# The halves of a weight tile made in pieces of 512 columns on GpSimd

## Time and profile before

| what | value |
|---|---|
| median of 3 runs | 2966.47 us (2964.6 to 2966.97) |
| the profiled execution | 2968.2 us, span 2966.2 us |
| mean granted TensorE clock | 0.987 |
| TensorE busy (matmuls) | 2858.6 us, 96% of the span |
| GpSimd busy | 1653.8 us, 56% |
| VectorE busy | 1540.7 us, 52% |
| ScalarE busy | 685.0 us, 23% |
| DMA | 285.48 MB, mean 96 GB/s |

### The profile page before, as it was taken

One profiled execution on the slowest core, in us unless ns is written; L12 is line 12 of the kernel. 1 busy time (PEld: TensorE's weight loads), 2 busy tenths in 40 slices (PEclk: granted clock), 3 DMA queues, 4 the chain that ended last, 5 costly groups with the idle time before them and its releaser, 6 DMA issues.

```text
span 2966.2 us, 44556 instructions
## 1 busy us (share of the span) xinstructions
PE 2858.6 (96%) x18104; PEld 2236.8 (75%) x18104; DVE 1540.7 (52%) x2279; ACT 685.0 (23%) x1169; POOL 1653.8 (56%) x1340
## 2 busy tenths in 40 slices
PE   4999998999999999999999999999999999899998
PEld 3666777888877767778888777777777777688786
DVE  5778776555224674444333375565465446462342
ACT  2444212000013442111000133233323333210001
POOL 3534567777765234576767744344435434566663
PEclk8999999999999999999999999999999999999999
DMA  7523543344323111232222221121111111222221
GB/s 242 162 101 120 181 166 136 128 153 145 131 96 92 34 59 65 70 115 81 96 99 99 101 67 54 53 69 66 48 59 69 67 53 67 78 85 92 92 100 57
DMA packets 102371, 285.48 MB, mean 96 GB/s; under 512 B 26030, under 2 KB 37038, under 8 KB 101934
## 3 DMA queue, kind: packets, MB, share of 16 engines
q1 hardware_dynamic: 85568, 274.75, 26.5%
q10 hardware_dynamic: 16622, 8.21, 1.2%
HBM read 280.76 MB, written 6.06 MB: 97 GB/s over the span
## 4 chain that ended last, share of the span: by engine, by line
PE 90%; DVE 6%; ACT 1%; issue 1%; DMA 1%; POOL 1%; ACTq 0%; DVEq 0%; SPq 0%; POOLq 0%
PE ps L334 26%; PE ps L336 24%; PE ps L335 24%; PE ps L1266 3%; PE ps L1088 3%; PE ps L1098 2%; PE ps L1108 2%; DMA raw<-in_weights_dram 1%; PE ps L1311 1%; DVE raw L1510 1%; PE ps L1408 1%; PE ps L1230 0%; PE ps L1388 0%; DVE mg L1657 0%; PE ps L1244 0%
## 5 line engine op out<-in xcount | busy, mean ns | idle before, releaser
L548 POOL TENSOR_TENSOR wR<-raw,wR 128x512 fp32r<-128x512 f32 (+1 forms) x866 | 1184.5, 1386 | 37.6
L544 POOL CAST wR<-raw 128x1024 fp32r<-128x1024 f32 (+4 forms) x470 | 475.1, 1011 | 1241.7 <-PE ps L336 1162.9
L334 PE MATMUL ps<-hR,wR 128*128 128x512 f32 x2320 | 946.2, 408 | 56.1 <-DVE hR L1552 26.7
L335 PE MATMUL ps<-hR,wR 128*128 128x512 f32 x2320 | 911.5, 393 | 0.0
L336 PE MATMUL ps<-hR,wR 128*128 128x512 f32 x2320 | 911.4, 393 | 0.0
L334 PEld LDWEIGHTS ps<-hR,wR 128*128 128x128 f32 x2320 | 440.0, 190 | 175.3 <-issue 59.0
L336 PEld LDWEIGHTS ps<-hR,wR 128*128 128x128 f32 x2320 | 439.5, 189 | 95.1
L335 PEld LDWEIGHTS ps<-hR,wR 128*128 128x128 f32 x2320 | 440.7, 190 | 87.9 <-issue 4.8
L1510 DVE CUSTOM_DVE_ANT_0 raw<-raw,cs 128x1024 f32<-128x1024 f32 x96 | 147.0, 1547 | 21.5 <-DMA raw<-in_weights_dram 13.9
L334 PE MATMUL ps<-act_f,wR 128*128 128x512 f32 x352 | 137.8, 391 | 0.0
L336 PE MATMUL ps<-act_f,wR 128*128 128x512 f32 x352 | 137.0, 389 | 0.0
(11 more groups left out here) (362 smaller groups left out, 3944.2 us busy)
## 6 DMA issues: line engine op xcount, KB each, us to landing
raw<-in_weights_dram SPq DMA_DIRECT2D x484, 512.0 KB, 3.3
raw<-in_weights_dram SPq DMA_DIRECT2D x50, 128.0 KB, 2.3
raw<-in_weights_dram SPq DMA_DIRECT2D x16, 256.0 KB, 2.6
bias_copies<-bias_rows ACTq DMA_DIRECT2D x2, 1905.0 KB, 9.1
bias<-bias_copies ACTq DMA_DIRECT2D x16, 224.0 KB, 7.2
raw<-in_weights_dram SPq DMA_DIRECT2D x8, 384.0 KB, 5.0
xT<-in_x_dram SPq DMA_DIRECT2D x1, 2048.0 KB, 9.2
out_dram<-xT SPq DMA_DIRECT2D x4, 512.0 KB, 2.7
```

The source lines that it names most:

```text
L334: mm(out, w_hi, r_hi, start=first, stop=False)
L335: mm(out, w_hi, r_lo, start=False, stop=False)
L544: nc.gpsimd.tensor_copy(wR[:, u, 0, 0:cols], raw[:, r % RING, 0:cols]).then_inc(hi_done, 1)
L548: ins = nc.gpsimd.tensor_tensor(wR[:, u, 1, part], raw[:, r % RING, part], wR[:, u, 0, part], ALU.subtract)
```

## The change

For each 512 columns of a tile, GpSimd first copies these columns (high half), waits for that copy, and subtracts (low half), and then goes on to the next 512 columns. A tile of more than 512 columns so takes copy, subtract, copy, subtract in place of copy, subtract, subtract. `hi_done` counts the pieces in place of the tiles. `tile_ready` is still signalled once, by the last subtraction.

```diff
@@ -536,15 +536,17 @@
         @block.gpsimd
         def _(pool):
 
+            halves = 0
             for g in range(G_USED):
                 u, cols, r = g % RING, ring_source(g)[2], RAW_AT["tile", g]
                 pool.wait_ge(raw_ready[r % RING], (r // RING + 1) * 16)
                 if g >= RING:
                     pool.wait_ge(tile_used, g - RING + 1)
-                nc.gpsimd.tensor_copy(wR[:, u, 0, 0:cols], raw[:, r % RING, 0:cols]).then_inc(hi_done, 1)
-                pool.wait_ge(hi_done, g + 1)
                 for first in range(0, cols, S):
                     part = slice(first, min(first + S, cols))
+                    nc.gpsimd.tensor_copy(wR[:, u, 0, part], raw[:, r % RING, part]).then_inc(hi_done, 1)
+                    halves += 1
+                    pool.wait_ge(hi_done, halves)
                     ins = nc.gpsimd.tensor_tensor(wR[:, u, 1, part], raw[:, r % RING, part], wR[:, u, 0, part], ALU.subtract)
                 ins.then_inc(tile_ready, 1)
```

## The result

| | before | after |
|---|---|---|
| median of ten runs each | 2966.72 us (2963.74 to 2971.85) | 2973.59 us (2968.47 to 2978.9) |
| ratio, 95% interval | | 1.0025 [1.0016, 1.0034] |
| the profiled execution, span | 2968.2, 2966.2 | 2978.4, 2976.4 |
| mean granted TensorE clock | 0.987 | 0.984 |

The change makes the kernel 6.9 us slower. I had forecast 2967.7 and a range up to 2972.5. The profiled execution of after is among the longest of its ten, so its lines carry some microseconds of scatter beside the effect. The ratio is formed from the single runs and not from the two medians (one of 3162 us in a later group of before is left out of it), so in what follows it can stand for a microsecond or so more or less than the difference of the medians.

A forecast was written before the change was run, and what follows sets the result against it. TensorE, busy 96% of the span, was taken to bound the kernel. The start's 1.0 us plus the merge's 0.2 made 1.2 us more, 2967.7 us as median (2969.4 for the profiled execution), range 2962.5 to 2972.5.

The forecast's parts named there:

- The start: First tiles, where GpSimd lets loads out: four pieces at 0.26 us, taken as 1.0 us slower, between 0 and 1.04.
- the merge: Layer 1's merge, 415 to 465 us, GpSimd and VectorE both full: five longer pairs, 1.3 - 1.1 = 0.2 us later.
- the 103 us: GpSimd's added time over the kernel, 396 tiles at 0.26 us, held to cost nothing outside the start and the merge.
- the norms: Where TensorE idles for VectorE: a margin of 1.7 us in the first FFN norm against 0.26, so no cost.
- the last `mg`: End of layer 1's merge: TensorE's 0.87 us idle for VectorE's last L1657, forecast near 1 us.
- The strict rule: Shared port as exclusive lock for the whole instruction: a merge pair of about 7.2 us, costing 1.2 us instead of 0.2.
- The lead of 0.78 us: In layer 1's merge, how far a tile was ready before TensorE loaded its weights; it would shrink and just last.
- The slower one: Rival, chance 0.14: GpSimd and VectorE stop overlapping in layer 1's merge, 3.7 us there, total 2971.2 or 2972.3.
- 6.96: Merge pair time in us at which the tiles' lead is used up and the slower rival decides; the forecast pair was 6.97.
- the 0.10: Chance of a loss beyond 5.9 us, from the slower rival and anything missed elsewhere of GpSimd's 103 us.
- The faster rival: Rival, chance 0.14: VectorE gets in sooner at the start and merge, 2.5 us faster, 2964.0, or 2961.5.
- The three that would prove me wrong: TensorE waiting over 1 us for subtractions, a merge pair over 7.2 us, a stretch after 470 us changing over 1 us.

The follow-up runs named there:

- e1: The changed kernel with only tiles 0 to 7 made in pieces, all others as before: 2972.64 us against 2967.08, ratio 1.0019.
- e12: The changed kernel with the first bias-row copy issued later, behind ScalarE's first rounding of h: 2968.7 us, ratio 1.001.
- e14: The kernel before, no pieces, with GpSimd memsets of 1024, 1024 and 512 columns ahead of tile 1: 2971.85 us against 2966.08, ratio 1.0021.
- e15: The kernel before, unchanged, run again for a second profile: 2966.96 us, ratio 1.0002.
- e4: The kernel before with the second bias-row copy moved behind the fifth attention step: 2968.58 us, ratio 1.0005.
- e11: The kernel before with the first bias-row copy issued later, behind ScalarE's first rounding of h: 2966.41 us against 2967.15, ratio 0.9999.
- e9: The kernel before with VectorE's bias masking in two halves, heads 2 and 3 only before the fifth attention step: 2970.2 us, ratio 1.001.
- e2: The changed kernel with only the tiles from 8 on made in pieces, the first 8 as before: 2968.7 us, ratio 1.0002.
- e6: The changed kernel with only tiles 0 to 3 made in pieces, all others as before: 2972.34 us against 2967.15, ratio 1.0014.
- e13: The kernel before, no pieces, with one GpSimd memset of 1024 columns ahead of tile 1: 2966.42 us against 2965.55, ratio 1.0001.

## Why the prediction was wrong, and where it was right

**The step that failed is "The start".** I priced four pieces at 0.26 us each, called 1.04 us an upper bound, and let "the loads behind it shift as a block". The start costs 5.6 us (e1). All three parts fell.
- The size of a piece. 0.26 us is the cost in an undisturbed stretch. At the start VectorE has operations ready, and a further boundary can let them in: tiles 0 and 1 take 1.25 us more in place of 0.52, tiles 4 to 7 some 1.5 (17.1 us in the mean of the six profiles that have them in pieces in this order, 15.6 in that of the nine that have them whole), where I had counted 0.52 for tiles 4 and 5 and nothing for 6 and 7. The load after tile 1 went out at 21.07 us, not at 20.4 (19.87 + 0.52).
- The bound. The Trainium skill, SBUF — State Buffer, section "SBUF: two separate sides", says that whichever engine starts first has the port pair for its whole instruction; the copy of 0.86 us in place of 0.40 and the subtraction of 1.59 in place of 0.73 agree. I had used this for the merge and in the two rivals, and not for the start, though the earlier trace rows showed VectorE held up there.
- The block. A load isn't simply as late as it was issued. One that slips by 1.2 us loses its lead over the first bias copy in most profiles (one of six still landed early, against four of seven), and then takes some 6 us longer to land. I had read a DMA share of 0.20 for 17 to 20 us, ahead of the load, and not what ScalarE puts on the DMA engines at 25 us, when the next one goes out. e12 takes a part of the loss away together with the copy, and e14 makes all of it by a slip alone. How much of the 5.6 us this term is stays open (below).

**The profile of before misled me too.** It was one of the executions in which the load is late already (24.51, 11.12 us). Read alone it says that a load there takes 11 us whatever happens. Nothing in one profile shows that this was one of two outcomes.

**What was right.** That GpSimd's lead covers nearly all of the 103 us; the cost of a piece where nothing disturbs it, and about GpSimd's busy time, 1737.5 us (about 1750 forecast); 866 copies, 800 of them of 512 columns; nothing lost in the steady stretches, 2832.5 us against 2831.6, with whole and split kernels within each other's scatter (2831.6 to 2834.4, the two with the mask moved aside); nothing to be seen at the norms; next to nothing in the merge, pairs of 6.85 us in the mean, the addition 0.43 us shorter, 0.3 us in sum against a forecast of 0.2.

**The merge was right by two errors that cancel.** I had written "no wait for a tile" and a wait for the last `mg` near 1 us. TensorE waited for tiles, 1.3 us more from the 2032nd matmul to the 2151st, and its 0.87 us for `mg` went away, which I had held for the lower bound. The strict rule would have made a pair 7.2 us. VectorE's L1512 does now meet a subtraction (2.01 us in place of 1.23), and one pair takes 7.16, but the mean is 6.85, so the rows don't bear out 7.2 for each pair. The lead of 0.78 us wasn't "the least of the whole trace" either. TensorE had waited for a tile of before outside the merge:

```profile
219.65 0.41 PE L334 MATMUL ps<-oT,wR 128*64 128x512 f32 x1 [1.02 <-POOL wR L548]
```

**The rivals.** The slower one gave a time near the measured one (2971.2 to 2972.3) at the wrong place: its mechanism, a VectorE operation let in at each new boundary, is what happens to tile 0. In the merge the lead did run out, but for 1.3 us in place of its 3.7, since pairs of 6.85 us in the mean stay under 6.96. That its number was so near is luck. So is the 0.10 that I had given to a loss beyond 5.9 us: I had hung it on the merge and on places that I might have missed, not on the start. The faster rival had its gain at the start, where there was a loss.

**The signs.** The three that would prove me wrong all came by the letter, and none points at the start. TensorE's matmuls waited for subtractions for 1.7 us in sum, over my limit of 1 us, but for 1.0 before already. One pair in the merge took over 7.2 us (7.72), but its counterpart did before too (7.22). The stretch from 883 to 1240 us of before takes 359.7 us after and 357.3 before, but e15, which is the kernel before, takes 359.2. For the start I had named the load after tile 1 at 20.4 us (21.07) and "everything after 110 us about 1 us later" (9.4 us at the 400th matmul in these two profiles). Both failed, and they point at the right place.

**What stays open.** The loss of 5.2 to 5.8 us from tiles 0 to 3 or from a delay follows the first product (34.3 or 40 us) up to the 200th matmul, but not to the 400th: e14's profile has the first product at 40.8 us and reaches the 400th matmul at 134.8, e4's has it at 34.4 and reaches it at 138.3. Between lie the loads of the bias and the wait at 105 us, and how these undo or double an early or late start wasn't separated. Nor is it shown that the race of the load with the copy makes most of the loss. With whole tiles a late landing puts the 200th matmul 4.7 us later (98.1 against 93.4 in the mean). If pieces raise the share of late landings from three of seven to five of six, that is 0.4 x 4.7 = 1.9 us of the 5.6, an estimate. And e11, where the load always should land early, gained 0.7 us, by its interval at most 3.0. The rest can be the slip itself and that of tiles 4 to 7. Nor was a slip of exactly 1.2 us tried without pieces; e14's was 2.1. And the shares of early and late landings rest on one profile for each kernel; e9's eleven times lie within 2.6 us of each other (2968.92 to 2971.47), too close for two outcomes 4.7 us apart.

## What to carry to other kernels

At the head of a kernel, where an engine's step lets the next load out, a sum of undisturbed durations is no upper bound: each new instruction boundary can let in the other engine that shares the port, and a slip can put a load behind a large transfer from another queue. List what other queues issue within a microsecond or two of the load that slips, and take a second profile of the same kernel before you trust a landing time there. Hundreds of extra pieces cost nothing that could be measured where GpSimd leads by a tile or more (e2), and four at the start cost 5 us (e6).

## What the runs showed of the hardware that I had not expected

- Added work can vanish: 0.95 us of memset ahead of a copy that would have waited for the port left the copy's end where it was (e13). The memset ran from 14.82 to 15.77 us, beside VectorE's operation on two SBUF tiles (L1503, 14.33 to 15.96), which took 1.63 us with it and without it. Against that, cutting tile 0 in pieces, 0.26 us of work, moved the end of tile 0 by 1.1 us (after).
- A 512 KB load landed 4.0 to 4.8 us after its issue without the 1905 KB DRAM to DRAM copy of another queue or 0.6 us and more ahead of it, and 9.6 to 11.1 us after it with less lead (4.3 us in one profile, with a lead of 0.51 us). In kernels with whole tiles, loads issued within 0.2 us of each other (24.31 to 24.51) came out both ways.
- Moving a copy of the whole bias out of this place gains nothing for the kernel before (e11, 0.9999), although it lands the load early: its 200th matmul starts at 92.7 us, but it takes 40.0 us from there to the 400th, and what is gained at 35 us is not in the end time.
